# A kernel of four layers: weight roundings before the stage that needs them, merged branches split pair by pair, and the input also handed over transposed

## The reference, cut to what matters

```python
# first layers, l = 0, 1
proj = x @ w_in[l] + b_in[l]                     # pool, q, k, v, iq, ik, iw, mq, gates
branches = (pool_branch(..), dsa_branch(..), memory_branch(..))   # 256 x 512 each
merged = sum(sigmoid(gate[n]) * (branches[n] @ w_br[l][n]) for n in range(3))
x = layer_norm(alpha * x + merged @ w_out[l], ln1_g[l], ln1_b[l])
x = layer_norm(alpha * x + moe(x, w_router, router_bias, w1[l], w3[l], w2[l]), ln2_g[l], ln2_b[l])
# second layers
z = rms(x, norm1) @ w_in_2                       # three kinds of attention read z
x = x + attended(z) @ w_out_2
x = x + relu(rms(x, norm2) @ w_ff1) ** 2 @ w_ff2 # 4096 hidden features
```

## Time and profile before

| engine | busy us | share of the span |
|---|---|---|
| PE (matmuls) | 1706.3 | 86% |
| DVE | 778.8 | 39% |
| ACT | 668.6 | 34% |
| POOL | 29.5 | 1% |

### The profile page before, as it was taken

How to read it: one execution, slowest core, us unless ns; L and a number is a source line. 1 busy time by engine, 2 the same in 40 slices (tenths; PEclk the granted TensorE clock), 3 DMA queues, 4 the chain that set the end, 5 groups by cost and what they waited for, 6 DMA issues and landing times.

```text
span 1995.5 us, 22133 instructions
## 1 busy us (share of the span) xinstructions
PE 1706.3 (86%) x9214; PEld 1268.4 (64%) x9214; DVE 778.8 (39%) x1480; ACT 668.6 (34%) x1077; POOL 29.5 (1%) x49
## 2 busy tenths in 40 slices
PE   6998987799887998987799985858899998588999
PEld 5777885443335777885443334744699887447997
DVE  4545343310115545343211015642455555515554
ACT  3336421111114336422111114442444444415443
POOL 4000000000000000000000000000000000000000
PEclk9998998799997999998799997976899998678999
DMA  8332445499994432345599992500255544003552
GB/s 260 131 126 103 148 148 211 183 421 421 421 420 174 145 125 105 148 148 211 195 421 421 421 421 106 199 30 1 104 184 187 176 145 176 0 21 127 190 190 105
DMA packets 57663, 392.67 MB, mean 197 GB/s; under 512 B 7124, under 2 KB 7168, under 8 KB 15696
## 3 DMA queue, kind: packets, MB, share of 16 engines
q1 hardware_dynamic: 54144, 380.30, 49.9%
q0 software_dynamic: 3264, 9.61, 1.5%
q10 hardware_dynamic: 144, 1.24, 0.2%
HBM read 390.07 MB, written 1.05 MB: 196 GB/s over the span
## 4 chain that ended last, share of the span: by engine, by line
PE 73%; DVE 10%; DMA 10%; ACT 5%; issue 2%; SPq 0%; DVEq 0%; ACTq 0%
PE psum L547 70%; DMA ring_sb<-in_weights 10%; PE psum L673 2%; ACT ring_rounded L1141 1%; DVE ring_rounded L1493 1%; PE psum L592 1%; ACT region_sb L1167 1%; DVE x_sb L1604 0%; ACT xT_hi_rounded L1376 0%; DVE x_sb L1602 0%; DVE region_sb L1881 0%; DVE region_sb L1884 0%; DVE small_sb L1877 0%; DVE region_sb L1875 0%; DVE small_sb L1590 0%
## 5 line engine op out<-in xcount | busy, mean ns | idle before, releaser
L547 PE MATMUL psum<-ring_sb,region_sb 128*64 128x512 f32 (+1 forms) x1728 | 433.4, 602 | 38.4 <-DMA ring_sb<-in_weights 24.4
L1493 DVE TENSOR_TENSOR ring_rounded<-ring_sb,ring_rounded 128x2048 fp32r<-128x2048 f32 (+4 forms) x152 | 321.4, 2131 | 243.9 <-ACT ring_rounded L1141 243.9
L547 PE MATMUL psum<-xT_hi_rounded,ring_rounded 128*128 128x256 f32 x1920 | 356.4, 287 | 0.0
L547 PEld LDWEIGHTS psum<-ring_sb,region_sb 128*64 128x64 f32 (+1 forms) x1728 | 151.1, 144 | 299.2 <-issue 282.2
L1141 ACT ACTIVATE ring_rounded<-ring_sb 128x2048 fp32r<-128x2048 f32 (+4 forms) x152 | 268.1, 1781 | 210.0 <-PE psum L547 148.8
L547 PE MATMUL psum<-ring_rounded,xT_hi_rounded 128*128 128x384 f32 (+4 forms) x960 | 277.9, 367 | 36.6 <-DVE ring_rounded L1493 17.6
L547 PE MATMUL psum<-xT_lo_rounded,ring_rounded 128*128 128x256 f32 x960 | 285.3, 297 | 27.8 <-DVE ring_rounded L1493 16.8
L547 PEld LDWEIGHTS psum<-xT_hi_rounded,ring_rounded 128*128 128x128 f32 x1920 | 306.8, 196 | 1.8 <-issue 0.5
L547 PEld LDWEIGHTS psum<-ring_rounded,xT_hi_rounded 128*128 128x128 f32 x960 | 184.1, 198 | 61.5 <-issue 39.7
L547 PEld LDWEIGHTS psum<-xT_lo_rounded,ring_rounded 128*128 128x128 f32 x960 | 188.9, 197 | 31.4 <-issue 18.1
L547 PE MATMUL psum<-ring_rounded,region_rounded 128*128 128x512 f32 x768 | 178.7, 392 | 3.0 <-DVE region_rounded L2083 3.0
(11 more groups left out here) (245 smaller groups left out, 1349.1 us busy)
## 6 DMA issues: line engine op xcount, KB each, us to landing
ring_sb<-in_weights SPq DMA_DIRECT2D x324, 1024.0 KB, 8.7
ring_sb<-in_weights SPq DMA_DIRECT2D x24, 768.0 KB, 4.3
ring_sb<-in_weights SPq DMA_DIRECT2D x8, 904.0 KB, 4.6
ring_sb<-in_weights SPq DMA_DIRECT2D x8, 900.0 KB, 4.6
ring_sb<-in_weights SPq DMA_DIRECT2D x8, 584.0 KB, 14.8
region_sb<-in_mem POOLq DMA_DIRECT2D x2, 1024.0 KB, 8.6
region_sb<-in_pool_band POOLq DMA_DIRECT2D x2, 1024.0 KB, 10.1
region_sb<-in_ln_g POOLq DMA_DIRECT2D x4, 512.0 KB, 4.7
```

Source lines behind the costliest of these rows:

```text
L547: return nc.tensor.matmul(dst, lhsT, rhs, start=first, stop=last, skip_group_check=True)
L1493: nc.vector.tensor_tensor(rounded(piece.raw), piece.raw, reread(piece.hi), ALU.subtract).then_inc(lo_made, 1)
```

## The change: what it does

1. A new input, `x_turned`, is x transposed by the host (128 x 8 x 256, 1 MB). SyncE loads it ahead of all else into an area that is free until later; ScalarE and VectorE make `xT_hi` and `xT_lo` of the first layer from it, and the 16 transposes of the first layer go. x itself is loaded behind the first five pieces. ScalarE issues the constants' load behind the four `xT_hi` roundings; TensorE waits for constants and bias just ahead of the first bias matmul, no longer ahead of its first instruction. GpSimd waits for the landing of pieces 2 and 3 ahead of its load of mem, and so of all that it loads later. VectorE computes the angles behind the third piece's rounding instead of behind the fifth's.
2. In both mixing stages `mergedT` is rounded pair by pair of chunks, the upper parts into `merged_upper`, the lower ones in place. Pair 0 is rounded behind (m, dc) = (2, 3), pair 1 behind dc = 5, pair 2 behind dc = 7, pair 3 at the end. Piece 38 of `w_out` is rounded at dc = 4, 39 at dc = 5, 40 at dc = 7 and 41 at the end.
3. In the norms after the experts, ScalarE rounds the next stage's first piece ahead of the square root and the second behind the centring; VectorE rounds the first piece between the shift and the gain.
4. In the second layers the first two pieces of `w_ff1` are rounded ahead of the additions to x, and ScalarE rounds the next layer's second piece already at the end of the feed-forward stage.

```diff
@@ tensor_mix
-            pe.wait_ge(consts_in, 16)
-            pe_turn_x(l, 0, [x_normed.at(l - 1, 2 + b) if l else (x_in, 32) for b in range(TB)])
+            if l:
+                pe_turn_x(l, 0, [x_normed.at(l - 1, 2 + b) for b in range(TB)])
...
-            pe_held(l, "mixed", xT, [merged_lo.at(l, c) for c in range(4)])
+            pe_held(l, "mixed", [merged_upper, mergedT], [merged_lo.at(l, c) for c in range(4)])
@@ scalar_mix
+            def split_merged(c):
+                a.wait_ge(*merged.at(l, 8 + 2 * c + 1))
+                nc.scalar.activation(rounded(merged_upper[:, 2 * c:2 * c + 2, :]), mergedT[:, 2 * c:2 * c + 2, :],
+                                     ACT.Copy).then_inc(merged_hi.sem, 1)
+
             def merge(m, dc):
-                if dc % 4 == 0:
-                    round_hi(first + 20 + m * 6 + dc // 4 * 3 + 6)
+                if m < 2 or dc < 4:
+                    if dc % 4 == 0:
+                        round_hi(first + 20 + m * 6 + dc // 4 * 3 + 6)
+                elif dc != 6:
+                    round_hi(first + 38 + (1, 2, 2, 3)[dc - 4])
                 act_merge(l, m, dc)
+                if m == 2 and dc > 2 and dc % 2:
+                    split_merged((dc - 3) // 2)
...
-            act_xT(l, 0)
+            if l:
+                act_xT(l, 0)
+            else:
+                a.wait_ge(turned_in, 16)
+                for c in range(0, KC, 2):
+                    nc.scalar.activation(rounded(xT[0][:, c:c + 2, :]), x_turned[:, c:c + 2, :], ACT.Copy).then_inc(xT_hi.sem, 1)
+                load(nc.scalar, consts[:, :], t["shape_consts"], consts_in)
...
+            split_merged(3)
             round_hi(first + 42)
-            for c in range(4):
-                a.wait_ge(*merged.at(l, 8 + 2 * c + 1))
-                a.wait_ge(*dense.of(("branch", l, 2, 7))[1])
-                nc.scalar.activation(rounded(xT[0][:, 2 * c:2 * c + 2, :]), mergedT[:, 2 * c:2 * c + 2, :], ACT.Copy).then_inc(merged_hi.sem, 1)
@@ scalar_second
+            up_first = first + 2 * len(Z2_CUTS) + 4
+            round_hi(up_first + 2)
             act_rms(l, 1, [res_added.at(l, n) for n in range(4)])
...
-            round_hi(up_first + 4 * D_FF // BANK)
+            round_hi(up_first + 4 * D_FF // BANK + 2 * (l + 1 < second_layers))
@@ vec_norm
             nc.vector.scalar_tensor_tensor(minus, moments[:, :, 0], -1.0, root, ALU.mult, ALU.mult).then_inc(ln_shifted.sem, 1)
+            round_lo(ahead)
@@ vector_mix
+            round_lo(first + 3)
+            if l == 0:
+                vec_angles()
             round_lo(first + 5)
             if l == 0:
-                vec_angles()
@@ pool_layer_inputs
             load(nc.gpsimd, bias_row, t["b_in"][l:l + 1, 0:C_MQ], bias_in.sem)
+            if l == 0:
+                for n in (2, 3):
+                    g.wait_ge(*ring.pieces[n].landed)
@@ the calls in order
+        load(nc.sync, x_turned, t["x_turned"], turned_in)
+        sync_weights()
         for b in range(TB):
             load(nc.sync, x[:, b, :], t["x"][0, b * P:(b + 1) * P, :], x_in)
-        load(nc.scalar, consts[:, :], t["shape_consts"], consts_in)
-        sync_weights()
...
-            vec_norm(l, 1, "experts")
+            vec_norm(l, 1, "experts", ring_first[l + 1] + 1)
+            round_hi(ring_first[l + 1] + 1)
             act_norm(l, 1)
+            round_hi(ring_first[l + 1] + 2)
```

More of the change, by code:

```diff
@@ L605, in pe_turn_x, with pe_rows @@
                     last.then_inc(full, 1)
-        def pe_rows(key, lhs, n, freed_by, ready, bias=None):
+        def pe_rows(key, lhs, n, freed_by, ready, bias=None, bias_ready=()):
             banks = [dense.take((*key, b), freed_by[b]) for b in range(TB)]
@@ L765, in cut @@
                 c0, c1 = Z_CUTS[n]
-                pe.wait_ge(*landed(bias_in, l, 1))
-                pe_rows(("z", l, n), xT, c1 - c0, [z_made.at(l, 2 * n + b) for b in range(TB)], xT_lo.at(l, 3), bias_row[:, c0:c1])
+                pe_rows(("z", l, n), xT, c1 - c0, [z_made.at(l, 2 * n + b) for b in range(TB)], xT_lo.at(l, 3), bias_row[:, c0:c1],
+                        [landed(bias_in, l, 1), (consts_in, 16)])
             def key_piece(n):
@@ L1681, in dsa_shares, with lower_merged @@
                 vec_shares("dsa", b, probs, DSA_HEADS, (b + 1) * P, dsa_shared)
+            def lower_merged(c):
+                v.wait_ge(*merged_hi.at(l, c))
+                nc.vector.tensor_tensor(rounded(mergedT[:, 2 * c:2 * c + 2, :]), mergedT[:, 2 * c:2 * c + 2, :],
+                                        reread(merged_upper[:, 2 * c:2 * c + 2, :]), ALU.subtract).then_inc(merged_lo.sem, 1)
             def merge(m, dc):
-                if dc % 4 == 0:
-                    round_lo(first + 20 + m * 6 + dc // 4 * 3 + 6)
-                vec_merge(l, m, dc)
-            vec_xT(l, 0)
+                if m < 2 or dc < 4:
+                    if dc % 4 == 0:
+                        round_lo(first + 20 + m * 6 + dc // 4 * 3 + 6)
+                elif dc != 6:
+                    round_lo(first + 38 + (1, 2, 2, 3)[dc - 4])
+                vec_merge(l, m, dc)
+                if m == 2 and dc > 2 and dc % 2:
+                    lower_merged((dc - 3) // 2)
+            if l:
+                vec_xT(l, 0)
+            else:
+                for n, c in enumerate(range(0, KC, 2)):
+                    v.wait_ge(*xT_hi.at(0, n))
+                    nc.vector.tensor_tensor(rounded(xT[1][:, c:c + 2, :]), x_turned[:, c:c + 2, :], reread(xT[0][:, c:c + 2, :]),
+                                            ALU.subtract).then_inc(xT_lo.sem, 1)
+            round_lo(first + 3)
+            if l == 0:
+                vec_angles()
             round_lo(first + 5)
             if l == 0:
-                vec_angles()
                 v.wait_ge(*router_hi_made.at(0))
@@ L1752, in vector_mix @@
                 merge(2, dc)
+            lower_merged(3)
             round_lo(first + 42)
[L1754 to L1757 removed]
             vec_norm(l, 0, "mixed")
@@ L2063, in vector_second @@
             fox_shares(1)
+            up_first = first + 2 * len(Z2_CUTS) + 4
+            round_lo(up_first + 2)
             for half in range(2):
```

20 lines of the change are left out of this document (10 added, 10 removed).

## The result

The changed kernel takes 1940.53 us (median of four runs, 1939.55 to 1943.74) beside 1997.39 (1995.09 to 2003.88). The ratio is 0.9721 with a 95% interval of 0.9704 to 0.9738: faster by 2.8%, or 57 us. The profiled execution took 1939.55, its span is 1938.1, its mean granted clock 0.924 (before 0.913). The forecast was 1932, with a range of 1923 to 1949.

What follows compares the result with a forecast made beforehand. PE's idle time and the slow clock behind it were taken as the bound. Terms 37.2 + 12 + 1.8 + 4.1 + 10.8 = 65.9 off 1996.95 gave 1931.0, as median 1932; 80% range 1923 to 1949.

Steps and rivals of the forecast that it cites:

- The mixing ends: End of both mixing stages: PE's two idles per layer and the slow clock behind them go, 37.2 us.
- the handover: Product at each mixing stage's end: a charge of 0.3 us a layer against the gain.
- (b): Mixing ends: only one of the two idles goes, 22 us less gain, 1954 us; chance 0.10.
- (d): Expert stages: bound by DMA, they give back the 37.2 us, 1969 us; chance 0.04.
- The start: Kernel start: earlier first product 6.5, idle before piece 5 and slow clock 7.1, less 1.5: 12 us, bounds 2 and 14.
- a GpSimd stream that now waits for piece 3 (landed about 12): Start: the router's weights, queued in this stream, land at 25 to 29, with no stall until 32.
- rival (a): Crowded start: constants after 17.5 stall PE, or router's weights past 32 keep the 4.31 idle; 1942 us, chance 0.15.
- ScalarE holds the router's and piece 5's rounding behind that cosine: Start: why PE idles 4.31 us at 45.90; earlier angles remove it and 2.8 us of slow clock.
- The norm entry and the second layers' entry: Norms after the experts: early roundings shorten PE's idles of 3.25 and 6.83, gaining 1.8 and 4.1 us.
- The feed-forward entries: Two feed-forward entries: PE starts at 1418.0 instead of 1423.42, 5.4 us each, 10.8 together.
- the slow clock behind it I leave as it is: Feed-forward entries: the slow clock following the idle was taken as unchanged, with no gain or loss counted.
- (c): Norms and feed-forward entries: an early rounding whose piece hasn't landed holds the norm itself; 2039 us, chance 0.02.

Runs made afterwards that it cites:

- e5: Kernel before with only the mixing stages' end changed (merged branches rounded by pairs, w_out pieces one by one); 1961.58 us, ratio 0.9834.
- e7: Kernel before with only the roundings of w_out spread, merged branches still rounded together at the end; 1976.28 us, ratio 0.9900.
- e8: Kernel before with only the merged branches rounded pair by pair, pieces 38 to 40 still rounded together; 1975.70 us, ratio 0.9897.
- e2: Changed kernel with GpSimd issuing the router's weights ahead of its wait for pieces 2 and 3; 1937.29 us, ratio 0.9719.
- e10: As e9, but GpSimd waits for pieces 6 and 7 instead of 2 and 3 before mem, bands and parameters; 1934.17 us, ratio 0.9691.
- e3: Changed kernel without GpSimd's wait for pieces 2 and 3; 1945.25 us, ratio 0.9752.
- e12: Kernel before with only the early roundings ahead of the two feed-forward entries; 1991.28 us, ratio 0.9974.
- e9: As e2, with x (1 MB) issued as GpSimd's last load; 1941.94 us, ratio 0.9725.

## Why the prediction was right, and where it was not

- **The mixing ends: right, mechanism and size.** 37.2 forecast, 36.1 in the trace (18.1 and 18.05), 36.7 in e5. e7 and e8 confirm that the two waits have one cause each. Each layer gave 0.5 less than forecast, and in the first all of it is in the product: it took 22.54, where 21.7 and 0.3 for the handover were forecast. Part of this is a count: of the 83 rows from which I took 0.226 a matmul one had begun ahead of the stretch, and 82 in 18.78 us make 22.0 for the 96. The other half microsecond isn't explained. The rivals that half the gain stays away (b) and that the expert stages give it back (d) fall.
- **The start: 12 forecast, 7.7 to 9.3 came.** The first step was right: x_turned is on chip at 5.70 (forecast 6.0) and PE starts at 11.24 (11.5). Two steps were wrong. First "a GpSimd stream that now waits for piece 3 (landed about 12)": piece 3 landed at 16.08, since pieces and constants were loaded side by side (the constants took 9.8 us to land, not 8.1), and the router's weights came at 34.5, not 25 to 29. That is rival (a)'s second condition, but not its price: PE idled 3.40 there, and 3 to 4 of the 12 went, not 10. Second, and this counts: I took "ScalarE holds the router's and piece 5's rounding behind that cosine" for the whole cause. e2 takes the router's wait away and PE waits as much elsewhere, for pieces 6 to 8. These pieces are slowed by the loads that are under way beside them, and only e10, which issues 3.3 MB and the small parameters behind pieces 6 and 7, comes near the 12. In the Trainium skill, DMA: Bandwidth & Descriptors, Issuing engines are not separate DMA queues, the transfers of all issuing engines share the 16 DMA engines. The traces agree: e3 and e10 change only what GpSimd issues and when (e10 x as well), and SyncE's pieces land later in e3 and sooner in e10. The forecast used this rule for the constants alone.
- **The norm entry and the second layers' entry: right.** 1.8 forecast and 1.8; 4.1 forecast and 4.6, since I charged 0.5 for VectorE's early rounding. It moved the gain behind it by 0.28 (1.75 us from the shift's start to the gain's, 1166.92 to 1168.67, where the kernel before has 1.47), and PE starts the moment that xT is complete:

```profile
595.05 0.61 PE L549 MATMUL psum<-ring_rounded,xT_hi_rounded 128*128 128x292 f32 x1 [1.41 <-DVE xT_lo_rounded L1520]
...
1179.11 0.69 PE L549 MATMUL psum<-ring_rounded,xT_hi_rounded 128*128 128x384 f32 x1 [1.84 <-DVE xT_lo_rounded L1899]
```

- **The feed-forward entries: right where they stand, wrong in the sum.** 5.4 forecast for each, 5.5 and 5.2 came, each idle 2.88 (forecast 3.0):

```profile
1366.83 0.58 PE L549 MATMUL psum<-xT_lo_rounded,ring_rounded 128*128 128x256 f32 x1 [2.88 <-DVE xT_lo_rounded L1899]
```

The step that failed is "the slow clock behind it I leave as it is". With the shorter idle the clock is granted at other times a stage later, and the last layer loses 5.5 us. Of the 8.5 us between forecast (65.9) and result (57.4), this is the larger part; the start's 3.7 and the mixing ends' 1.1 add to it, and 0.5 more at the second layers' entry and 0.6 and 0.5 unasked in the feed-forward stages work against it. In the Trainium skill, TensorE: Matmul & The Clock Gate, What's actually happening, the clock is said to be set by how busy TensorE has been recently. The stretch of 5.83 us with PE busy throughout at 0.50 shows that busy time as the profile counts it isn't enough to tell where the clock falls. What decides it there stays open: the profiles show that the loss comes with the shorter idle (e12 changes only the roundings ahead of the feed-forward entries), none shows what lies between.
- **Slower (c): fell.** No early rounding held a norm; ScalarE's roundings ahead of the square roots (578.09 and 1155.01) waited for no landing.
- **The number.** 1940.5 lies in the range of 1923 to 1949, but just outside the 1925 to 1940 that I gave the forecast itself, and near the 1942 of rival (a), which is luck: (a) was to lose 10 us at the start, and the start lost less than half of that, the clock in the last layer most of the rest.

## What to carry to other kernels

On an in-order engine, put a rounding of weights behind the last instruction that PE needs before that piece can have landed, not ahead of a whole group of them: here that was worth 8 us a layer, and with the merged branches rounded in pairs 18. When a wait at a kernel's start is to be taken away, look first at what is loaded beside the next pieces, and at how busy the DMA engines are with it, not at its megabytes alone. Here they were full, so the wait only moved, and what helped was to ask later for what is used later. A shorter idle period of PE need not be worth its length, since the clock can take some back elsewhere: here 11 us of idle were worth 5, so measure such a cut by the whole kernel and not by the wait that it removes.

## What the runs showed of the hardware that I had not expected

- The granted clock can fall inside a stretch in which PE is busy: in the changed kernel it was 0.99 from 1667.00 to 1670.17 and 0.50 for the next 5.83 us (40 instructions); the kernel before ran the same instructions (39 on record) in 3.19 us at 1.00.
- It can also stay at 0.50 while PE is busy without a break: from 28.37 to 41.00 in e9, 12.63 us.
- Such a fall repeats from run to run and from kernel to kernel: seven profiles of six kernels give 151.5 to 151.7 us for the same stage, at spans from 1930 to 1993 us.
- A load of 64 KB took 15.8 us to land in the changed kernel, behind 2.3 MB issued from the same engine, and 8.1 to 9.8 when issued ahead of them (e2, e9, e10).
- Small loads take DMA engines out of proportion to their bytes: in e9, 0.42 MB in 671 packets took 83.8% of the engines' time from 32 to 41 us.
